# The first tokens' first four FFN tiles turned, rounded and subtracted between the last two output groups

## The chip, the cores and the metric

The kernel runs on one core of a Trainium2 chip. The metric is the time of one execution on the device, in microseconds (us). TensorE multiplies matrices into PSUM, whose eight banks are `bank[0]` to `bank[7]`; VectorE, ScalarE and GpSimd do the rest; SyncE (SP) issues the DMAs. Each engine works through its own queue in order, and the queues meet at semaphores alone. Called "granted clock" below is the share of TensorE's full clock that the chip let through.

## The reference

256 tokens of width 1024 in float32 go through two blocks. The first has three mixing branches and 32 experts; the second is attention and a gated feed-forward layer (FFN). The change lies between the last two steps of the second block:

```python
def second_block(x, g_pre_mix, g_post_mix, w_qkv, w_o, rel_bias, g_pre_ffn, g_post_ffn, w_gate, w_up, w_down):
    for i in range(DEPTH):
        h = rms_norm_2(x, g_pre_mix[i])
        ...
            m = chunk_relpos_attention(h, w_qkv[i], w_o[i], rel_bias[i // N_MIXERS])
        ...
        x = x + rms_norm_2(m, g_post_mix[i])
        h = rms_norm_2(x, g_pre_ffn[i])
        x = x + rms_norm_2(swiglu(h, w_gate[i], w_up[i], w_down[i]), g_post_ffn[i])
    return x

def rms_norm_2(x, g):
    xf = x.astype(jnp.float32)
    y = xf * lax.rsqrt(jnp.mean(xf * xf, axis=-1, keepdims=True) + RMS_EPS)
    return (y * g.astype(jnp.float32)).astype(x.dtype)

def swiglu(h, w_gate, w_up, w_down):
    return (jax.nn.silu(h @ w_gate) * (h @ w_up)) @ w_down
```

## The kernel before, in words

Tokens are split into two halves, i = 0 (first tokens) and i = 1 (second tokens), 128 each. Every float32 product is made of three faster ones: each operand is the sum of a rounded part ("hi", written by ScalarE) and a remainder ("lo", a subtraction by VectorE), and the product keeps hi x hi, lo x hi and hi x lo. Weights stream in pieces of 128 x 1024; `split_to(n)` splits the pieces up to number n, on ScalarE a cast (L1543, "wh"), on VectorE a subtraction (L1969, "wl"). Four pieces are held at a time, so a split also waits until TensorE is done with an older piece.

**The output product.** `o_tile(k, parts)` multiplies tile k of the attention's result with the rows k of `w_o`. A part (i, c) is the token half i and the column half c (512 columns); it sums into `bank[2 * c + i]` over the eight tiles, three matmuls of 512 columns for each (L782). The first tokens' parts are made first, tile by tile beside the attention. What is left at the end are tiles 5, 6 and 7 for the second tokens: nine matmuls for (1, 0), then nine for (1, 1) (L1412 to L1414).

**The norm and the sum.** For each part ScalarE squares the bank (L1552, with a read of the accumulator), VectorE multiplies the bank with the gain (`gained`, L2514). Once both column halves of a token half are squared, ScalarE adds their sums (`mean`, L1560), and GpSimd makes the factor (L2690, L2692). VectorE then adds the normed part to the residual X (`added`, L2521).

**The turn.** X is turned so that features lie on the partitions: `turn_ffn(i, tiles)` on TensorE turns 128 x 128 tiles (L1424) into the banks named by `FFN_BANK`, one tile each, and before tiles 0 and 4 it waits for `added` of the column half they lie in. ScalarE rounds each tile with the FFN's gain (L1914, "hi ffn"), VectorE subtracts (`low_ffn`, L2505, "lo ffn"). The norm of the FFN's input is applied later, to the products.

**The first gate product.** `first_gate` makes the first two of the FFN's gate groups: the first tokens' half tile by tile (`gate_half(0, ...)`, two matmuls of 256 columns, L1441), each behind "lo ffn" of its tile, then the second tokens' half (four matmuls, L1441 and L1445). The other turns stand between them as the table `later` says: the first tokens' tiles 5 to 7 behind gate tile 1, the second tokens' tiles 0 to 3 behind gate tile 5, and so on. Ahead of the gate half stand five turns and a filler, `warm(WARM[2], 4)`: six matmuls of a constant into bank 4, 12 records in the profile (L745). Then come the up product (`joint`, L848 and L851) and ten more chunks of the FFN.

The order on the other engines is written out by hand. ScalarE: the squares of (0,0) and (0,1), a mean, the square of (1,0), `split_to(q_o + 2)`, the square of (1,1), a mean, the roundings of the eight tiles of the first tokens, `split_to(q_o + 3)`, the roundings of the second tokens (q_o is the last piece of `w_o`; q_o + 1 and q_o + 2 hold the first gate group's weights). VectorE, in `add_normed`: gained (0,0), gained (0,1), added (0,0), gained (1,0), added (0,1), gained (1,1), four subtractions, added (1,0), four subtractions, added (1,1), then the second tokens' subtractions with the splits. Here the first index is the token half.

Of the kernel before, what the change touches and what calls it, by code (L numbers as in the profile page):

```python
# [13 lines left out]
ACT = mybir.ActivationFunctionType  # L14
AX = mybir.AxisListType.X

P = 128
# [13 lines left out]
WARM = (10, 1, 6, 10, 2, 6, 12)  # L31
FFN_BANK = ((0, 2, 6, 7, 1, 3, 0, 2), (6, 7, 1, 3, 0, 2, 3, 1))
# [13 lines left out]
G_MIX, G_MEM, G_Q, G_KV, G_POOL, G_MIX2, G_FFN2, G_ROUTE, G_FIN, G_EXP, G_END = np.cumsum([0, 8, 8, 3, 2, 4, 8, 8, 8, 8, 8]).tolist()  # L46
# [24 lines left out]
class Points:  # L71
# [10 lines left out]
    def up(self, name, *key):  # L82
        if name not in self.sems:
            self.sems[name] = self.semaphore("p_" + name.replace(" ", "_"))
        n = self.count[name] = self.count.get(name, 0) + 1
        assert self.real or (name, key) not in self.value, (name, key)
        self.value[name, key] = n
        self.latest = (self.sems[name], n)
        return self.sems[name], 1

    def at(self, name, *key):
        return (self.sems[name], self.value[name, key]) if self.real else (None, 1)
# [236 lines left out]
def program(nc, ctx, x, xT, mem, memT, positions, gate_b, grow, w_route, b_route, rel_ext, cst, out, wt, dense,  # L329
# [402 lines left out]
    def tensor(e, real):  # L732
# [8 lines left out]
        def warm(n, b, src=None):  # L741
            src = C if src is None else src
            enter(b)
            for _ in range(n):
                e.matmul(bank[b][:, 0:P], src[:, 0:P], src[:, 0:P], start=True, stop=True)  # L745
# [645 lines left out]
        def o_tile(k, *parts):  # L1391
            wide(wt.run["o", k // 2][k % 2], "gained o", (mT[0][:, k, :], mT[1][:, k, :]), k == 0, k == 7,
                 at("finished", "r", k), *parts)
# [15 lines left out]
            for k, i in HALVES_AT.get(step, ()):  # L1409
                o_tile(k, ((i, 0), (i, 1)))  # L1410
        o_tile(7, ((0, 0), (0, 1)))
        for c in range(2):  # L1412
            for k in (5, 6, 7):
                o_tile(k, ((1, c),))  # L1414


        def turn_ffn(i, *tiles):

            for k in tiles:
                b = FFN_BANK[i][k]  # L1420
                enter(b, "lo", "ffn", k, i)
                if k % 4 == 0:
                    e.wait_ge(*at("added", "o", i, k // 4))
                e.transpose(bank[b][:, P * i:P * i + P], X[:, i, P * k:P * k + P], ident).then_inc(*up("turn", "ffn", k, i))  # L1424

        def token_half(v, i):
            return v.rearrange("p (z n) -> p z n", z=2)[:, :, P * i:P * i + P]
# [22 lines left out]
        def first_gate():  # L1450

            later = {(0, 1): (0, 5, 6, 7), (0, 5): (1, 0, 1, 2, 3), (1, 0): (1, 4, 5, 6, 7)}
            turn_ffn(0, 0, 1, 2, 3, 4)
            warm(WARM[2], 4)
            for i in range(2):
                for q in wt.run["fg", 0]:
                    for kk in range(wt.pieces[q].rows):
                        gate_half(i, q, kk)
                        step = (i, wt.pieces[q].k0 + kk)
                        if step in later:  # L1460
                            turn_ffn(*later[step])
# [66 lines left out]
    def scalar(e, real):  # L1528
        split, limit_q = [0], [LATE]

        def split_to(n):

            while split[0] <= min(n, limit_q[0] - 1):
                q = split[0]
                p = wt.pieces[q]
                if p.first == 0:
                    e.wait_ge(*landed(p.unit))
                if q == LATE:
                    for u in under_split.values():
                        e.wait_ge(*released(u))  # L1540
                if q >= PIECES:
                    e.wait_ge(*at("piece", max(z for z in range(q) if wt.place(z) == wt.place(q))))
                e.copy(halves(q)[0], piece_view(q)).then_inc(*up("wh", q))  # L1543
                split[0] += 1
# [345 lines left out]
        for step, _ in enumerate(attention("r", 16, 384, causal_exps("r"), r_finish, 6, PT4)):  # L1890
# [6 lines left out]
            if step == 10:  # L1897
                whole(fill)
        q_o = wt.run["o", 3][1]
        for i in range(2):  # L1900
            for c in range(2):
                if (i, c) == (1, 1):
                    split_to(q_o + 2)
                e.wait_ge(*(at("piece", q_o) if (i, c) == (1, 1) else at("piece", q_o, i, c)))
                if (i, c) != (0, 0):
                    e.wait_ge(*own())
                square(rms("o")[0][:, 2 * c + i:2 * c + i + 1], bank[2 * c + i][:, :], junk, "o", c, i, scale=1 / 32)
            mean("o", i)


        for i in range(2):
            for k in range(8):
                e.wait_ge(*at("turn", "ffn", k, i))
                e.activation(hT[0][:, k, P * i:P * i + P], bank[FFN_BANK[i][k]][:, P * i:P * i + P], ACT.Copy,  # L1914
                             scale=G[:, G_FFN2 + k:G_FFN2 + k + 1]).then_inc(*up("hi", "ffn", k, i))
            if i == 0:
                split_to(q_o + 3)
        for i in range(2):
            e.wait_ge(*at("added", "o", i, 1))
            e.wait_ge(*(at("squared", "ffn", 0) if i else at("squared", "o", "mean", 1)))  # L1920
# [39 lines left out]
    def vector(e, real):  # L1960
        split, limit_q = [0], [LATE]

        def split_to(n):

            while split[0] <= min(n, limit_q[0] - 1):
                q = split[0]
                h, l = halves(q)
                e.wait_ge(*at("wh", q))
                e.tensor_tensor(l, piece_view(q), h.bitcast(F), ALU.subtract).then_inc(*up("wl", q))  # L1969
                split[0] += 1  # L1970
# [529 lines left out]
        def low_ffn(i, tiles):  # L2500

            sl = slice(P * i, P * i + P)
            for k in tiles:
                e.wait_ge(*at("hi", "ffn", k, i))
                e.scalar_tensor_tensor(hT[1][:, k, sl], bank[FFN_BANK[i][k]][:, sl], G[:, G_FFN2 + k:G_FFN2 + k + 1],  # L2505
                                       hT[0][:, k, sl].bitcast(F), ALU.mult, ALU.subtract).then_inc(*up("lo", "ffn", k, i))

        def add_normed(name, row, ready):

            e.wait_ge(*ready)  # L2510

            def gained(i, c):
                e.wait_ge(*at("squared", name, c, i))
                e.tensor_tensor(H[:, i, 512 * c:512 * c + 512], bank[2 * c + i][:, :],  # L2514
                                gb[:, row, 512 * c:512 * c + 512], ALU.mult).then_inc(*up("gained " + name, i, c))

            def added(i, c):
                xs = X[:, i, 512 * c:512 * c + 512]
                e.wait_ge(*at("gained " + name, i, c))
                e.wait_ge(*at("factor", name, i))  # L2520
                e.scalar_tensor_tensor(xs, H[:, i, 512 * c:512 * c + 512], rms(name)[1][:, i:i + 1], xs, ALU.mult,  # L2521
                                       ALU.add).then_inc(*up("added", name, i, c))

            gained(0, 0)
            gained(0, 1)
            added(0, 0)
            gained(1, 0)
            added(0, 1)
            gained(1, 1)
            if name == "o":  # L2530
                low_ffn(0, range(4))
            added(1, 0)
            if name == "o":
                low_ffn(0, range(4, 8))
            added(1, 1)
# [244 lines left out]
```

## Time and profile before

| | |
|---|---|
| median of 3 runs | 764.17 us (763.53 to 764.65) |
| profiled execution, its time | 765.39 us |
| its span, first to last instruction | 763.5 us |
| mean granted clock | 0.993 |
| TensorE busy | 728.5 us, 95% |
| VectorE busy | 417.9 us, 55% |
| ScalarE busy | 338.3 us, 44% |

The span is the time from the first to the last instruction; some 1.9 us of the profiled time lie outside. A row of the line of time gives start, duration, engine, line, operation, output and inputs by the program's names, the shape and how many instructions were merged; in brackets how long the engine stood before and what ended that. TensorE's matmuls overlap: the next one starts before the last one's recorded end, so distances between starts say more than recorded lengths.

### The profile page before, as it was taken

To read this page: it belongs to the slowest core of one execution; us is meant where nothing else is said; L and a number is where in the kernel's file an instruction comes from. 1 tells how busy PE (TensorE), PEld (TensorE's weight loads), DVE (VectorE), ACT (ScalarE), POOL (GpSimd) and SP (SyncE) were. 2 spreads that over 40 slices of the span, in tenths; PEclk is the share of its full clock that TensorE was granted. 3 is DMA by queue.
4 is the path that set the end of the run, shared out by engine and by line. 5 is a ranking of instruction groups with operands and counts; after the bars stand their busy time and mean duration, and the time that the engine had idled before them with its cause. 6 is when DMAs were issued, how large, how long until landed. Compare 5 with 4: busy or idle time off the path is not lost.

```text
span 763.5 us, 12333 instructions
## 1 busy us (share of the span) xinstructions
PE 728.5 (95%) x5082; PEld 596.0 (78%) x5082; DVE 417.9 (55%) x740; ACT 338.3 (44%) x605; POOL 32.8 (4%) x66
## 2 busy tenths in 40 slices
PE   9999999999999999999787789999999999999997
PEld 8998987888888866666455459998778888888885
DVE  5677656677666511111010118676568867676766
ACT  5966665554443521111010137555667453444343
POOL 1700000000000000000000001000001000000001
PEclk9999999999999999999999999999999999999999
DMA  8963667438989999999999997954234555545101
GB/s 333 418 232 120 227 212 283 174 128 319 364 320 346 377 412 420 422 426 424 427 424 424 419 415 313 419 176 161 111 111 166 192 194 178 209 170 209 62 1 55
DMA packets 30281, 206.05 MB, mean 270 GB/s; under 512 B 3600, under 2 KB 3984, under 8 KB 11408
## 3 DMA queue, kind: packets, MB, share of 16 engines
q1 hardware_dynamic: 30224, 205.25, 68.7%
q8 instruction: 41, 0.67, 0.4%
q14 instruction: 16, 0.13, 0.1%
HBM read 204.18 MB, written 1.05 MB: 269 GB/s over the span
## 4 chain that ended last, share of the span: by engine, by line
PE 87%; DMA 6%; ACT 2%; DVE 2%; issue 1%; POOL 0%; SPq 0%; DVEq 0%; POOLq 0%; ACTq 0%
PE ps L782 44%; PE ps L848 10%; DMA ext<-in_dense 6%; PE ps L1210 6%; PE ps L851 5%; PE ps L1231 3%; PE ps L1132 3%; PE ps L1241 2%; PE ps L888 1%; PE ps L1046 1%; PE ps L1356 1%; ACT big L1804 1%; PE ps L1370 1%; PE ps L1331 1%; PE ps L1261 1%
## 5 line engine op out<-in xcount | busy, mean ns | idle before, releaser
L1969 DVE TENSOR_TENSOR whl<-raw,whl 128x1024 fp32r<-128x1024 f32 (+4 forms) x182 | 213.0, 1189 | 127.6 <-ACT whl L1543 126.0
L1543 ACT CAST whl<-raw 128x1024 fp32r<-128x1024 f32 (+4 forms) x182 | 181.9, 1020 | 68.7 <-PE ps L782 46.7
L782 PE MATMUL ps<-whl,fra 128*128 128x512 f32 (+2 forms) x858 | 198.7, 387 | 0.0
L782 PEld LDWEIGHTS ps<-whl,fra 128*128 128x128 f32 x858 | 156.7, 188 | 30.4 <-issue 1.0
L848 PE MATMUL ps<-fra,whl 128*128 128x512 f32 x336 | 105.5, 395 | 0.0
L782 PE MATMUL ps<-whl,frb 128*128 128x512 f32 x360 | 84.9, 390 | 0.0
L782 PEld LDWEIGHTS ps<-whl,frb 128*128 128x128 f32 x360 | 66.6, 188 | 13.2
L851 PEld LDWEIGHTS ps<-fra,whl 128*128 128x128 f32 x336 | 63.1, 188 | 14.8
L782 PE MATMUL ps<-fra,whl 128*128 128x256 f32 x552 | 69.5, 285 | 0.0
L782 PEld LDWEIGHTS ps<-fra,whl 128*128 128x128 f32 x552 | 67.1, 191 | 0.8 <-issue 0.7
L851 PE MATMUL ps<-fra,whl 128*128 128x256 f32 x336 | 66.0, 278 | 0.0
L848 PEld LDWEIGHTS ps<-fra,whl 128*128 128x128 f32 x336 | 51.8, 189 | 0.7
L1210 PE MATMUL ps<-ext,big 128*32 128x256 f32 x320 | 46.6, 402 | 1.5 <-DMA big<-in_w_gate_e 1.4
L2398 DVE TENSOR_TENSOR S<-S,ps 128x256 f32<-128x256 f32 x6 | 2.5, 421 | 82.7 <-ACT S L1818 82.7
L1210 PE MATMUL ps<-raw,big 128*32 128x256 f32 x380 | 40.9, 389 | 7.0 <-DMA ext<-in_dense 3.8
L1210 PE MATMUL ps<-big 128*32 128x256 f32 x240 | 41.4, 396 | 4.1 <-DMA ext<-in_dense 4.1
L1818 ACT ACTIVATE S<-ps 128x256 f32<-128x256 f32 x6 | 2.3, 384 | 89.9 <-PE ps L1210 89.9
L1210 PEld LDWEIGHTS ps<-raw,big 128*32 128x32 f32 x380 | 21.4, 112 | 16.6 <-issue 9.9
L2547 DVE TENSOR_REDUCE S<-ps 128x256 f32<-128x512 f32 x44 | 28.2, 683 | 4.2 <-PE ps L851 4.2
L1617 ACT ACTIVATE S<-S,st 128x128 f32<-128x128 f32 (+1 forms) x48 | 21.5, 450 | 16.1 <-DVE st L2052 16.1
L1210 PEld LDWEIGHTS ps<-ext,big 128*32 128x32 f32 x320 | 22.6, 116 | 7.2 <-issue 2.8
L1210 PEld LDWEIGHTS ps<-big 128*32 128x32 f32 x240 | 19.9, 114 | 10.4 <-issue 5.8
(300 smaller groups left out, 856.9 us busy)
## 6 DMA issues: line engine op xcount, KB each, us to landing
raw<-in_dense SPq DMA_DIRECT2D x79, 1024.0 KB, 5.2
ext<-in_dense SPq DMA_DIRECT2D x11, 2048.0 KB, 24.2
raw<-in_dense SPq DMA_DIRECT2D x5, 2048.0 KB, 31.1
ext<-in_w_down_e SPq DMA_DIRECT2D x8, 1024.0 KB, 9.5
big<-in_w_gate_e SPq DMA_DIRECT2D x7, 1024.0 KB, 27.3
big<-in_dense SPq DMA_DIRECT2D x3, 2048.0 KB, 29.1
raw<-in_dense SPq DMA_DIRECT2D x2, 3072.0 KB, 33.2
raw<-in_w_gate_e SPq DMA_DIRECT2D x5, 1024.0 KB, 7.6
```

The source lines that it names most:

```text
L782: t = e.matmul(o, a, w, start=first and n == 0, stop=final and n == 2, skip_group_check=not check)
L848: e.matmul(bank[b][:, :], h[:, kk, cols[j]], hT_both[:, k], start=(k == 0), stop=(k == 7), skip_group_check=True)
L851: t = e.matmul(bank[b][:, 0:256], l[:, kk, cols[j]], hT[0][:, k], start=False, stop=(k == 7), skip_group_check=True)
L888: t = e.matmul(bank[j // 2][:, 256 * (j % 2):256 * (j % 2) + 256], w[:, kk, P * j:P * j + P], y[:, k], start=(n == k == j % 2 == 0), stop= ...
L1132: t = e.matmul(bank[2 + a][:, P * (kk % 4):P * (kk % 4) + P], H[:, i, P * kk:P * kk + P], hot[:, P * i:P * i + P], start=(i == 0), stop=(i ...
L1210: t = e.matmul(bank[0][32 * j:32 * j + 32, 256 * half_:256 * half_ + 256], XE[:, kk, 32 * j:32 * j + 32], expert_rows(key, 4 * g + j, kk), ...
L1231: t = e.matmul(bank[2 + c][32 * j:32 * j + 32, :], hidden(g)[1][:, P * k + 32 * j:P * k + 32 * j + 32], slot_view(wt.raws["ed", 4 * g + j] ...
L1241: t = e.matmul(turned(k), rows_out(g, k // 4)[:, P * (k % 4):P * (k % 4) + P], CM, start=False, stop=False, skip_group_check=True)
L1543: e.copy(halves(q)[0], piece_view(q)).then_inc(*up("wh", q))
L1617: t = e.activation(s, s, ACT.Exp, bias=mx(h)[:, i:i + 1], scale=-1.0, accum_out=sums(h)[0][:, i:i + 1])
L1969: e.tensor_tensor(l, piece_view(q), h.bitcast(F), ALU.subtract).then_inc(*up("wl", q))
L2547: e.tensor_reduce(dst[:, j, :], bank[b][:, :].rearrange("p (z n) -> p n z", z=2), AX, ALU.add).then_inc(*up("summed " + name, c, j))
```

## The change

Four of the five turns of the first tokens move from behind the output parts to between (1,0) and (1,1), the fifth stays behind (1,1), and the filler is gone. On ScalarE the four roundings move ahead of the square of (1,1), and the split of piece q_o + 2 moves from ahead of that square to behind the rounding of the fifth tile. On VectorE the four subtractions move ahead of the gained product of (1,1). Nothing that is computed changes, except that the six filler matmuls, whose result nobody reads, are left out.

```diff
@@ TensorE
         o_tile(7, ((0, 0), (0, 1)))
-        for c in range(2):
-            for k in (5, 6, 7):
-                o_tile(k, ((1, c),))
...
+        for c in range(2):
+            if c:
+                turn_ffn(0, 0, 1, 2, 3)
+            for k in (5, 6, 7):
+                o_tile(k, ((1, c),))
...
             later = {(0, 1): (0, 5, 6, 7), (0, 5): (1, 0, 1, 2, 3), (1, 0): (1, 4, 5, 6, 7)}
-            turn_ffn(0, 0, 1, 2, 3, 4)
-            warm(WARM[2], 4)
+            turn_ffn(0, 4)
@@ ScalarE
+        def high_ffn(k, i):
+            e.wait_ge(*at("turn", "ffn", k, i))
+            e.activation(hT[0][:, k, P * i:P * i + P], bank[FFN_BANK[i][k]][:, P * i:P * i + P], ACT.Copy,
+                         scale=G[:, G_FFN2 + k:G_FFN2 + k + 1]).then_inc(*up("hi", "ffn", k, i))
+
         for i in range(2):
             for c in range(2):
                 if (i, c) == (1, 1):
-                    split_to(q_o + 2)
+                    for k in range(4):
+                        high_ffn(k, 0)
...
-        for i in range(2):
-            for k in range(8):
...
-            if i == 0:
-                split_to(q_o + 3)
+        high_ffn(4, 0)
+        split_to(q_o + 2)
+        for k in range(5, 8):
+            high_ffn(k, 0)
+        split_to(q_o + 3)
+        for k in range(8):
+            high_ffn(k, 1)
@@ VectorE
             added(0, 1)
-            gained(1, 1)
             if name == "o":
                 low_ffn(0, range(4))
+            gained(1, 1)
             added(1, 0)
```

## Rows read from the trace of the kernel before

**Rows 1.** The page, part 1: busy time, share of the span and instructions of each engine

```profile
PE 728.5 (95%) x5082; PEld 596.0 (78%) x5082; DVE 417.9 (55%) x740; ACT 338.3 (44%) x605; POOL 32.8 (4%) x66
```

**Rows 2.** TensorE's waits, whole run: us in total, times, longest

```profile
PE ps L1210 <- DMA ext<-in_dense: 7.8, 2, 4.1
...
PE ps L1441 <- DVE fra L2505: 0.3, 2, 0.2
```

**Rows 3.** The waits of all engines from 580 us to the end

```profile
POOL st L2690 <- ACT junk L1552: 172.6, 2, 172.1
```

**Rows 4.** The chain that ended last: start, us, what

```profile
571.39 0.69 DVE H L2514
```

**Rows 5.** TensorE's line of time, 560 to 584 us: start, us, what

```profile
563.52 7.12 PE L782 MATMUL ps<-whl,fra 128*128 128x512 f32 x30
570.48 0.71 PE L1424 MATMUL ps<-C,X 128*128 128x128 f32 x5
571.02 1.50 PE L745 MATMUL ps<-C 128*128 128x128 f32 x12
572.49 0.71 PE L1441 MATMUL ps<-fra,whl 128*128 128x256 f32 x4
...
574.18 0.71 PE L1441 MATMUL ps<-fra,whl 128*128 128x256 f32 x4 [0.18 <-DVE fra L2505]
...
575.97 0.47 PE L1441 MATMUL ps<-fra,whl 128*128 128x256 f32 x2 [0.17 <-DVE fra L2505]
```

**Rows 6.** VectorE's line of time, the same stretch

```profile
568.45 0.75 DVE L2521 SCALAR_TENSOR_TENSOR X<-H,st,X 128x512 f32<-128x512 f32 x1 [0.36 <-POOL st L2692]
...
569.96 0.74 DVE L2521 SCALAR_TENSOR_TENSOR X<-H,st,X 128x512 f32<-128x512 f32 x1
571.39 0.69 DVE L2514 TENSOR_TENSOR H<-ps,gb 128x512 f32<-128x512 f32 x1 [0.69 <-ACT junk L1552]
...
573.03 0.74 DVE L2521 SCALAR_TENSOR_TENSOR X<-H,st,X 128x512 f32<-128x512 f32 x1
573.69 1.12 DVE L2505 SCALAR_TENSOR_TENSOR fra<-ps,C,fra 128x128 fp32r<-128x128 f32 x4
574.73 0.74 DVE L2521 SCALAR_TENSOR_TENSOR X<-H,st,X 128x512 f32<-128x512 f32 x1
575.47 1.13 DVE L2505 SCALAR_TENSOR_TENSOR fra<-ps,C,fra 128x128 fp32r<-128x128 f32 x4
```

**Rows 7.** ScalarE's line of time, the same stretch

```profile
567.40 0.29 ACT L1560 ACTIVATE st<-st 128x1 f32<-128x1 f32 x1
...
571.39 0.29 ACT L1560 ACTIVATE st<-st 128x1 f32<-128x1 f32 x1
571.59 1.38 ACT L1914 ACTIVATE fra<-ps,C 128x128 fp32r<-128x128 f32 x5
...
574.12 1.06 ACT L1543 CAST whl<-raw 128x1024 fp32r<-128x1024 f32 x1
575.05 1.16 ACT L1914 ACTIVATE fra<-ps,C 128x128 fp32r<-128x128 f32 x4
```

**Rows 8.** TensorE's line of time in the expert stage, two places

```profile
400.49 0.42 PE L1210 MATMUL ps<-raw,big 128*32 128x256 f32 x3 [1.68 <-DMA big<-in_w_gate_e]
...
443.81 0.47 PE L1219 MATMUL ps<-C,S 128*128 128x128 f32 x2 [1.05 <-DVE S L2398]
445.73 0.66 PE L1261 MATMUL ps<-ext,S 128*32 128x256 f32 x4 [1.45 <-issue]
```

**Rows 9.** Stretches: us, busy by engine, PEclk (granted clock), DMA share, GB/s

```profile
397.00:401.00 4.00, 2.33 (x21) 1.68 (x23) 0.00 (x0) 0.00 (x0) 0.00 (x0) 1.00 1.01 428
410.00:416.00 6.00, 4.90 (x64) 2.79 (x64) 0.00 (x0) 0.00 (x0) 0.00 (x0) 0.72 0.99 418
442.50:449.50 7.00, 4.50 (x51) 2.44 (x47) 0.42 (x1) 1.50 (x4) 0.00 (x0) 0.76 1.00 415
570.00:577.00 7.00, 6.65 (x52) 6.03 (x51) 6.31 (x18) 5.67 (x18) 0.56 (x1) 1.00 0.01 2
```

More of the change, by code:

```diff
@@ L1908, in scalar @@
             mean("o", i)
-        for i in range(2):
-            for k in range(8):
-                e.wait_ge(*at("turn", "ffn", k, i))
-                e.activation(hT[0][:, k, P * i:P * i + P], bank[FFN_BANK[i][k]][:, P * i:P * i + P], ACT.Copy,
-                             scale=G[:, G_FFN2 + k:G_FFN2 + k + 1]).then_inc(*up("hi", "ffn", k, i))
-            if i == 0:
-                split_to(q_o + 3)
+        high_ffn(4, 0)
[5 more added lines that the diff above has]
+            high_ffn(k, 1)
         for i in range(2):
```

## The prediction, made before the changed kernel was built or run

> **What bounds the kernel now.** I read the page first. TensorE is busy 728.5 us of 763.5 [rows 1], so whatever moves its work at this place moves the end, unless a wait further on takes it back. The list of TensorE's waits over the whole run has the two waits of this stage at 0.3 us together, on the subtraction at L2505 [rows 2]. The same list for 580 us to the end has no row of TensorE at all; its rows are other engines that wait, the first ones shown [rows 3]. So from 580 us on TensorE runs without waiting for anybody, and a shift that exists at 580 arrives at the end unchanged. The chain that ended last shows who sets the time in the stage itself: behind the 30 output matmuls of TensorE, which end at 563.52 + 7.12 = 570.64 [rows 5], and a square on ScalarE it goes on VectorE from 571.39 [rows 4] until the second tokens' gate matmuls start.
>
> TensorE's line of time gives the shapes [rows 5]. Its matmuls are recorded with 0.27 to 0.39 us each but overlap, so I count from start to start. 30 output matmuls take 570.48 - 563.52 = 6.96 us, 0.232 each; 9 of them are one column half of the last three tiles, 2.09 us. So the half for the second tokens and the first 512 columns, called (1,0), hands over at 570.48 - 2.09 = 568.39, and (1,1) at 570.48. Five turns take 571.02 - 570.48 = 0.54, 0.108 each. The second tokens' gate matmuls, which need everything, start at 575.97: that is the point I measure the change at.
>
> VectorE sets that point [rows 6]: from the gained product of (1,1) at 571.39, four subtractions, the addition at 573.03, four subtractions from 573.69, the addition at 574.73, the first subtraction of the second tokens at 575.47, and 0.50 later TensorE. Four subtractions with the next start cost 574.73 - 573.69 = 1.04; an addition before a subtraction costs 573.69 - 573.03 = 0.66 or 575.47 - 574.73 = 0.74.
>
> **The change, part by part.**
>
> The wait in front of the first turn. The four turns for the first tokens now stand between (1,0) and (1,1), and the first waits for the addition (0,0) on VectorE. That addition starts at 568.45 and takes 0.75 [rows 6]: it ends at 569.20. Nothing ahead of it changes: it follows ScalarE's mean at 567.40 [rows 7] by 1.05 us over GpSimd's root. TensorE answers to a VectorE result about 0.15 after its end (the subtraction that starts at 573.69 ends some 0.35 later and lets the gate matmul start at 574.18; 0.49 in all, once more 0.50 at 575.47 [rows 5, 6]). So the turns start at 569.35, and not at 568.39: 0.96 us of new standing time, with nine output matmuls, (1,1), queued behind the waiting turn. The banks that the turns write are free by then.
>
> The turns. Four times 0.108 = 0.43. (1,1) therefore starts at 569.78 and hands over at 571.87 instead of 570.48: 1.39 later. On the path it costs all of that, because ScalarE's square of (1,1), the mean, GpSimd's root and the gained product hang on its last matmul.
>
> The filler and the turns that went. The 12 matmul records from 571.02 to 572.49 are gone [rows 5]. I cost this at nothing either way: they lie beside the first four subtractions, the first gate matmul started at 572.49 when the first of these had just ended, and TensorE stands anyway ahead of 574.18 and of 575.97.
>
> The moved subtractions. The first four now run ahead of the gained product of (1,1). They follow the addition (0,1) at 569.96 [rows 6], from about 570.6 to 571.7, time in which VectorE would now be standing; their roundings on ScalarE (0.25 each, from about 569.7) are ahead of them. This takes 1.03 us (four of about 0.26) out of the chain behind (1,1). That is the gain of the change, and its cover is complete.
>
> A wait that comes up. With the four subtractions gone from behind the gained product, the addition (1,0) comes to its factor too early. For the first tokens the addition followed the mean by 568.45 - 567.40 = 1.05 [rows 6, 7]. The mean of the second tokens moves from 571.39 to 572.78 [rows 7]; so the addition starts at 573.83, not at 573.4 when VectorE is free: 0.4 us of the 1.03 are lost again.
>
> The sum. Mean 572.78, addition (1,0) 573.83, fifth subtraction 574.49, addition (1,1) 575.53, first subtraction of the second tokens 576.27, gate matmul of the second tokens 576.77. Before it was 575.97: **+0.80 us**. By terms: +0.96 wait, +0.43 turns, -1.03 subtractions, +0.44 for the factor. TensorE itself doesn't set it: after (1,1) come one turn and the gate matmuls of four tiles with three turns until about 573.3, it then stands until 574.98 (fifth subtraction at 574.49 and 0.49), works 1.4 us, and stands again from 576.4.
>
> ScalarE's moved cast. The cast of 1024 columns for the second piece after the last output tile (L1911) stood ahead of the square of (1,1), and now stands behind it. From the mean at 572.78: 0.20 to the fifth rounding (571.59 - 571.39), 0.25, cast 0.93 (575.05 - 574.12), three roundings 0.75, second cast 0.93 [rows 7]: the first rounding of the second tokens starts at 575.84 and ends 0.37 later, at 576.21. The subtraction that needs it would start at 576.27. The cover is 0.06 us; without it, if both casts held ScalarE for their full 1.06, the path would be 0.2 longer. I take nothing, and keep the 0.2 for the range. The subtraction of the same piece on VectorE stays behind the second tokens' four subtractions, so it moves with the rest, and so does the release of its buffer: TensorE meets the piece with the same slack. SP's queue issues nothing in this stretch that TensorE waits for [rows 3].
>
> What a turn costs in a stream: the row gives 0.108 each for five in a row [rows 5]. The Trainium skill, "TensorE: Matmul & The Clock Gate", Part 4: PE-mode transpose, has about 275 ns for one in the context of a kernel; the recorded length here, 0.27, agrees with it, and the distance between two does not. With 0.275 for each of the four, my estimate would be 0.67 longer, +1.5 us.
>
> **The rivals.**
>
> A, the wait in front of the turns isn't there, or the change doesn't hold what it says: if the turns found their addition done, the shift of (1,1) would be 0.43 alone, and the sum 0.43 - 1.03 + 0.44 = -0.16: 764.0 us. If the factor weren't late either, -0.6: 763.6. Against it: the addition's start at 568.45 has its cause in work that isn't touched. Even this case stays within 0.2%; to be faster by more than that, 1.5 us would have to go from a chain of which at most 1.03 is moved.
>
> B, the clock falls (the side of slower). The granted clock was 1.00 in this stage [rows 9], which is the level of 2.4 GHz, and the filler is gone, with two new standing times of 1.0 and 1.7 us. Elsewhere it fell to 1.2 GHz: around 411, behind the longest wait of TensorE, 4.1 us for a transfer [rows 2, 9], and around 445, where it had only two identity matmuls at 443.81 between waits of 1.05 and 1.45 us [rows 8, 9]. Against it: ahead of 400.49 it stood 1.68 us between column-tiled matmuls and kept 1.00 [rows 8, 9]. In the new stretch from 573.3 to 576.8 it would have eight gate matmuls and four turns, which is more than at 443.81 and not far from the other. A fall costs this: 6 us at a mean of 0.72 is 6 x 0.28 = 1.7 us of full-clock work [rows 9]. It decides if the stretch with the 1.7 us wait counts as rest: then 0.80 + 1.7 = +2.5 us, 766.7 us, and less if the fall meets time in which TensorE stands.
>
> The Trainium skill speaks against this change here, in the same section: in transpose mode the array isn't counted as busy the way it is in a matmul. By that, the eleven turns between the output and the second gate half keep nothing up, and B is likelier. The trace's fall at 445, around two such short matmuls, doesn't contradict it.
>
> C, ScalarE becomes the bound: the two casts at 1.06 and roundings that wait for the turns put 0.2 to 0.5 on the sum: 765.2 to 765.5 us.
>
> D, the shift is absorbed later: 764.2 us. Against it: no wait of TensorE after 580 [rows 3].
>
> **How the numbers follow.** The sum is made in the profiled execution: 765.39 us, of which the span is 763.5; +0.80 makes 766.2 there. The median of the runs is 764.17, 1.2 below the profiled one, and +0.80 gives 764.97. Chances: the forecast 0.58, C 0.14, A with D 0.14, B 0.14. A difference of 0.2%, 1.5 us, is about what a measurement of this kernel can tell from no change. The forecast, A, C and D lie inside it; the three runs before spread over 1.1 us, so some of the forecast's chance goes to each side. Faster 0.05, same 0.77, slower 0.18. The range takes A's 763.9 or so, C and half of B: 763.8 to 766.5.
>
> **What would show it.** In the changed kernel: TensorE's first turn at about 569.35 behind a wait on the addition at L2521; (1,1)'s square on ScalarE at about 572.05; the addition (1,0) behind GpSimd at 573.8; the first gate matmul with the fifth tile at about 575.0; the second tokens' gate half at 576.8; the same clock as before. A gate half before 576 would make the forecast wrong; so would a stretch of half clock after 573, or a wait of TensorE after 580 that was not there.

## The result

The changed kernel takes 765.65 us in the median of 11 runs (764.47 to 768.85) against 764.09 of 11 runs before; the ratio is 1.0021, with a 95% interval of 1.0011 to 1.0031. Measured again beside other kernels it was 1.0009 (0.9998 to 1.0021) and 1.0016 (1.0006 to 1.0025). So it is slower, by 0.1 to 0.2%. The profiled execution took 765.13 us with a span of 763.2.

All distances below are from one mark, the start of VectorE's first addition, (0,0), to the second tokens' first gate matmul. Everything ahead of the mark is the same in both programs. TensorE's line of time after the change answers to [rows 5]; the turns stand at L1419 now and the gate matmuls at L1443. The first row ends with the half (1,0):

```profile
562.38 5.07 PE L782 MATMUL ps<-whl,fra 128*128 128x512 f32 x21
568.21 0.63 PE L1419 MATMUL ps<-C,X 128*128 128x128 f32 x4 [0.76 <-DVE X L2528]
568.60 2.31 PE L782 MATMUL ps<-whl,fra 128*128 128x512 f32 x9
570.75 0.27 PE L1419 MATMUL ps<-C,X 128*128 128x128 f32 x1
570.78 0.71 PE L1443 MATMUL ps<-fra,whl 128*128 128x256 f32 x4
572.41 0.55 PE L1419 MATMUL ps<-C,X 128*128 128x128 f32 x3 [0.92 <-DVE H L2521]
...
573.87 0.71 PE L1443 MATMUL ps<-fra,whl 128*128 128x256 f32 x4 [0.44 <-DVE fra L2512]
...
575.67 0.47 PE L1443 MATMUL ps<-fra,whl 128*128 128x256 f32 x2 [0.17 <-DVE fra L2512]
```

VectorE, which answers to [rows 6] (addition L2528, gained product L2521, subtraction L2512):

```profile
567.32 0.75 DVE L2528 SCALAR_TENSOR_TENSOR X<-H,st,X 128x512 f32<-128x512 f32 x1 [0.36 <-POOL st L2699]
...
568.82 0.74 DVE L2528 SCALAR_TENSOR_TENSOR X<-H,st,X 128x512 f32<-128x512 f32 x1
569.48 1.12 DVE L2512 SCALAR_TENSOR_TENSOR fra<-ps,C,fra 128x128 fp32r<-128x128 f32 x4
571.67 0.69 DVE L2521 TENSOR_TENSOR H<-ps,gb 128x512 f32<-128x512 f32 x1 [1.07 <-ACT junk L1553]
572.71 0.75 DVE L2528 SCALAR_TENSOR_TENSOR X<-H,st,X 128x512 f32<-128x512 f32 x1 [0.35 <-POOL st L2699]
573.38 1.12 DVE L2512 SCALAR_TENSOR_TENSOR fra<-ps,C,fra 128x128 fp32r<-128x128 f32 x4
574.41 0.74 DVE L2528 SCALAR_TENSOR_TENSOR X<-H,st,X 128x512 f32<-128x512 f32 x1
575.18 1.12 DVE L2512 SCALAR_TENSOR_TENSOR fra<-ps,C,fra 128x128 fp32r<-128x128 f32 x4
```

ScalarE, which answers to [rows 7] (mean L1561, roundings L1903, square L1553, casts L1544):

```profile
566.27 0.29 ACT L1561 ACTIVATE st<-st 128x1 f32<-128x1 f32 x1
...
568.55 1.14 ACT L1903 ACTIVATE fra<-ps,C 128x128 fp32r<-128x128 f32 x4 [0.37 <-PE ps L1419]
570.95 0.60 ACT L1553 ACTIVATE junk<-ps 128x512 f32<-128x512 f32 x1 [1.25 <-PE ps L782]
...
571.67 0.29 ACT L1561 ACTIVATE st<-st 128x1 f32<-128x1 f32 x1
...
572.12 1.04 ACT L1544 CAST whl<-raw 128x1024 fp32r<-128x1024 f32 x1
...
573.82 1.06 ACT L1544 CAST whl<-raw 128x1024 fp32r<-128x1024 f32 x1
574.75 1.16 ACT L1903 ACTIVATE fra<-ps,C 128x128 fp32r<-128x128 f32 x4
```

GpSimd, the factor of the second tokens:

```profile
572.04 0.56 POOL L2699 TENSOR_TENSOR st<-st 128x1 f32<-128x1 f32 x1 [3.56 <-ACT st L1561]
```

Two cuts of the span say where the time is. First the kernel before, then the changed one, each from the mark to the second gate half and from there to the end (us; busy time of TensorE, its weight loads, VectorE, ScalarE, GpSimd; granted clock, DMA share, GB/s):

```profile
568.45:575.97 7.52, 7.17 (x50) 6.29 (x49) 6.68 (x16) 6.63 (x19) 0.78 (x2) 1.00 0.01 2
575.97:763.50 187.53, 181.84 (x976) 156.29 (x976) 135.03 (x160) 83.58 (x105) 5.06 (x9) 1.00 0.40 146
```

```profile
567.32:575.67 8.35, 6.06 (x38) 4.97 (x38) 6.77 (x16) 6.52 (x19) 0.78 (x2) 1.00 0.01 2
575.67:763.20 187.53, 181.83 (x976) 156.27 (x976) 135.08 (x160) 83.55 (x105) 5.05 (x9) 1.00 0.40 146
```

The stretch grew from 7.52 to 8.35 us (8.36 before its two ends are rounded, as in the table below), and the rest is 187.53 us in both. Nothing of the shift is taken back in the 187 us that follow, and nothing is added. The span as a whole is 0.3 us shorter in this execution, because the mark came at 567.32 instead of 568.45. That difference lies ahead of the first changed instruction; in the later profiles, of whatever kernel, the mark stood anywhere from 566.60 to 569.68. A reader who compares two spans here compares the expert stage of two executions. A reader who measures from the mark gets the distance of the changed kernel again to 0.01 us, in every repeat below.

### The profile page after: what moved, and what is told of

It is laid out like the page before. It is cut to its first block, busy times and chain, and to the rows that moved or that the text cites. A ratio compares the mean times of both kernels' runs of the same rounds, so it can differ in the third digit from the quotient of the medians.

```text
span 763.2 us, 12309 instructions
## 1 busy us (share of the span) xinstructions
PE 727.2 (95%) x5070; PEld 594.9 (78%) x5070; DVE 417.9 (55%) x740; ACT 338.1 (44%) x605; POOL 32.2 (4%) x66
## 4 chain that ended last, share of the span: by engine, by line
PE 85%; DMA 8%; SPq 3%; ACT 1%; issue 1%; DVE 1%; POOL 0%; DVEq 0%; POOLq 0%; ACTq 0%
PE ps L782 45%; PE ps L848 10%; DMA ext<-in_dense 5%; PE ps L851 5%; PE ps L1210 5%; DMA raw<-in_w_up_e 2%; SPq L609 2%; PE ps L1241 2%; PE ps L1231 2%; PE ps L1132 2%; PE ps L888 2%; PE ps L1046 1%; PE ps L1356 1%; PE ps L1331 1%; PE ps L1370 1%
## 5 line engine op out<-in xcount | busy, mean ns | idle before, releaser
L1544 ACT CAST whl<-raw 128x1024 fp32r<-128x1024 f32 (+4 forms) x182 | 181.8, 1019 | 68.4 <-PE ps L782 46.6
L1210 PE MATMUL ps<-ext,big 128*32 128x256 f32 x320 | 48.2, 414 | 1.6 <-DMA big<-in_w_gate_e 1.5
L1210 PE MATMUL ps<-raw,big 128*32 128x256 f32 x380 | 42.5, 398 | 6.4 <-DMA ext<-in_dense 3.9
```

The lines of the kernel that those rows point to most:

```text
L1210: t = e.matmul(bank[0][32 * j:32 * j + 32, 256 * half_:256 * half_ + 256], XE[:, kk, 32 * j:32 * j + 32], expert_rows(key, 4 * g + j, kk), ...
```

## The experiments

Two theories are set against each other in what was expected of each run. Theory W: the waits and turns alone make the loss. Theory C: the granted clock falls in this stage because the filler is gone. Every run was read in the same way; the distance from the mark, in us, with the start of the square of (1,1) and of the addition (1,0) after the mark. Each distance is that of the one profiled execution:

| run | what | distance | square (1,1) | addition (1,0) | ratio to before (95%) |
|---|---|---|---|---|---|
| before | | 7.52 | 2.22 | 4.58 | |
| after | the change | 8.36 | 3.63 | 5.40 | 1.0021 (1.0011 to 1.0031) |
| a4_after | the same again | 8.36 | 3.63 | 5.40 | 1.0009 (0.9998 to 1.0021) |
| c2_after | the same again | 8.37 | 3.64 | 5.40 | 1.0016 (1.0006 to 1.0025) |
| b5_tensor | TensorE's part alone | 8.91 | 3.63 | 5.99 | 1.0019 (1.0009 to 1.0029) |
| a2_late | turns two tiles later | 7.61 | 2.88 | 4.64 | 1.0012 (0.9999 to 1.0024) |
| a3_bare | before, no filler | 7.49 | 2.22 | 4.58 | 0.9997 (0.9987 to 1.0006) |
| a1_fill | filler, too much of it | 8.99 | 3.64 | 5.40 | 1.0017 (1.0006 to 1.0027) |
| c1_fill | filler that fits | 8.37 | 3.64 | 5.40 | 1.0019 (1.0010 to 1.0028) |
| b3_cast | cast at its old place | 9.13 | 4.44 | 6.20 | one run |
| b4_back | two subtractions back | 8.39 | 3.64 | 5.49 | one run |
| b1_two | two tiles early | 7.27 | 2.52 | 4.36 | 1.0001 (0.9990 to 1.0011) |
| c3_three | three tiles early | 7.46 | 2.78 | 4.54 | one run |
| d1_length | the change, filler elsewhere | 8.36 | 3.63 | 5.40 | 1.0016 (1.0006 to 1.0026) |

The time from the second gate half to the end was 187.51 to 187.54 us in every one of them.

**The change again.**

> The changed kernel once more, as the mark for the other runs of this batch. The distance from the start of the addition (0,0) on VectorE to the second tokens' first gate matmul was 7.52 us before and 8.35 us in the changed kernel. Theory W (waits alone): 8.35 again and +0.8 us in time. Theory C (the clock falls here in some executions, because the filler is gone): the distance is 8.35 in most executions and the time is +1.5 us, with single executions 2 us or more above the rest.

> The changed kernel a third time, as the mark for the next one. Theory W: distance 8.36 us, time 0.84 us (0.11%) over before; the three measurements together should lie around 1.001. Theory C: nearer to 1.002.

The distance is 8.36 and 8.37. The times don't choose between the two theories by themselves: 1.0009 and 1.0016.

**TensorE's part alone.** Before, with this alone:

```diff
+        for c in range(2):
+            if c:
+                turn_ffn(0, 0, 1, 2, 3)
+            for k in (5, 6, 7):
+                o_tile(k, ((1, c),))
...
-            turn_ffn(0, 0, 1, 2, 3, 4)
-            warm(WARM[2], 4)
+            turn_ffn(0, 4)
```

> The change on TensorE alone: four turns between the last two output groups, no filler, but ScalarE and VectorE in their order of before (roundings behind the square of (1,1), subtractions behind its gained product). Theory W (the sum of the prediction): the wait and the turns stay on the path, 0.96 + 0.43, and nothing comes back, so the distance from the addition (0,0) to the second tokens' gate half is 7.52 + 1.39 = 8.91 us, 0.55 more than in the changed kernel, and the time is 1.4 us (0.18%) over before. A rival that has the loss come from the new order on ScalarE and VectorE expects it at or under 8.36.

8.91 us, as expected to the hundredth. VectorE has its four subtractions between the gained product and the addition again (b5_tensor, L2514, L2505, L2521), and the addition doesn't wait for the factor:

```profile
570.95 0.69 DVE L2514 TENSOR_TENSOR H<-ps,gb 128x512 f32<-128x512 f32 x1 [2.10 <-ACT junk L1552]
571.55 1.12 DVE L2505 SCALAR_TENSOR_TENSOR fra<-ps,C,fra 128x128 fp32r<-128x128 f32 x4
572.59 0.74 DVE L2521 SCALAR_TENSOR_TENSOR X<-H,st,X 128x512 f32<-128x512 f32 x1
```

So TensorE's part costs 1.39 and the new order on VectorE and ScalarE gives 0.55 back: the addition (1,0) comes 0.59 earlier, which is the four subtractions (1.03) less what is lost to the factor (0.44), and 0.04 of that goes again at ScalarE's cast, which the section on the prediction works out.

**The turns two tiles later.** The changed kernel with

```diff
-            if c:
-                turn_ffn(0, 0, 1, 2, 3)
             for k in (5, 6, 7):
+                if (c, k) == (1, 7):
+                    turn_ffn(0, 0, 1, 2, 3)
                 o_tile(k, ((1, c),))
```

> The changed kernel with the four turns two tiles later: behind tiles 5 and 6 of the last column half instead of ahead of tile 5. The addition they wait for is then done 0.4 us before TensorE comes to them. Theory W: the standing time of 0.96 us goes, the last output matmul ends 0.43 later than before the change instead of 1.39, and the distance is 7.52 + 0.43 - 1.03 + 0.44 = 7.36 us, 0.99 less than in the changed kernel and 0.16 less than before it; time 1.0 us under the changed kernel. Theory C: the same distance, and a time that still lies 0.5 us or more above before, since the long wait ahead of the fifth gate tile and the missing filler stay.

The wait is gone: TensorE's row has no standing time in front of the turns, and the distance falls by 0.75. But 0.25 of the expected 0.99 didn't come. TensorE, then ScalarE (a2_late):

```profile
568.93 0.60 PE L1419 MATMUL ps<-C,X 128*128 128x128 f32 x4
```

```profile
569.24 1.14 ACT L1903 ACTIVATE fra<-ps,C 128x128 fp32r<-128x128 f32 x4 [0.79 <-PE ps L1419]
570.47 0.60 ACT L1553 ACTIVATE junk<-ps 128x512 f32<-128x512 f32 x1
```

The instruction behind the last output matmul starts at 570.07, 2.48 us after the mark at 567.59, and the square could start 0.2 later, at 2.67. It starts at 2.88: ScalarE is still in the four roundings that stand ahead of it in its queue (569.24 + 1.14 = 570.38). Work put ahead of a wait is free only where it ends before the wait does; in the changed kernel it did, because TensorE's own wait had held the square back anyway.

**The filler.** Two ways to look at the clock. Before without its filler:

```diff
             turn_ffn(0, 0, 1, 2, 3, 4)
-            warm(WARM[2], 4)
```

> The kernel before without its filler ahead of the gate product, nothing else changed. Theory W: the filler lay under the wait for the first subtraction, so the distance stays 7.5 us and the time is that of before within 0.1 us. Theory C: the distance stays, and the time rises by 0.5 us or more in the median, with slow single executions.

Distance 7.49, ratio 0.9997, granted clock 1.00 in the stage. The filler of the kernel before bought nothing here; its own price was 0.03 us. And the changed kernel with filler ahead of the turns and of the first tokens' fifth gate tile:

```diff
             if c:
+                warm(3, 4)
                 turn_ffn(0, 0, 1, 2, 3)
...
                     for kk in range(wt.pieces[q].rows):
+                        if (i, wt.pieces[q].k0 + kk) == (0, 4):
+                            warm(6, 6)
                         gate_half(i, q, kk)
```

> The changed kernel with filler under its two new waits: 3 filler matmuls (0.7 us) ahead of the four turns and 6 (1.5 us) ahead of the first tokens' fifth gate tile, both shorter than the waits they lie under (0.94 and 1.7 us). Theory W: nothing changes, distance 8.3 to 8.4, time as the changed kernel within 0.1 us. Theory C: the distance is the same, but the time comes down by 0.7 us to +0.8 us over before, and the slow single executions go.

This one missed: the distance grew to 8.99. The wait of 1.7 us under which the six matmuls were to lie doesn't exist at that place (a1_fill, TensorE and ScalarE):

```profile
573.17 1.50 PE L745 MATMUL ps<-C 128*128 128x128 f32 x12
574.43 0.72 PE L1444 MATMUL ps<-fra,whl 128*128 128x256 f32 x4
574.99 0.60 PE L1419 MATMUL ps<-C,X 128*128 128x128 f32 x4
```

```profile
575.30 1.14 ACT L1906 ACTIVATE fra<-ps,C 128x128 fp32r<-128x128 f32 x4 [0.53 <-PE ps L1419]
```

The filler keeps TensorE until 574.43, the gate matmuls follow at once with no wait, and the second tokens' turns come so late that ScalarE waits 0.53 us for them. In the changed kernel's rows the reason can be read: TensorE stands at 572.41, for 0.92 us, and what ends it is the gained product of (1,1), not the subtraction. The turn of tile 5 writes bank 3, and bank 3 holds the output half (1,1) until VectorE has read it. Only 0.44 us of standing are left at the fifth gate tile. With filler sized by these rows, against the run above:

```diff
-                            warm(6, 6)
+                            warm(2, 6)
                         gate_half(i, q, kk)
                         step = (i, wt.pieces[q].k0 + kk)
+                        if step == (0, 1):
+                            warm(4, 6)
                         if step in later:
                             turn_ffn(*later[step])
```

> The changed kernel with filler that fits under each of its new waits as the trace has them: 3 matmuls ahead of the four turns (0.7 us under 0.94), 4 ahead of the turn of the sixth tile (1.0 under 1.1), 2 ahead of the fifth gate tile (0.5 under 0.7). Theory W: distance 8.4 us, time within 0.1% of the changed kernel in this batch. Theory C: distance the same, time 0.5 us or more under the changed kernel.

```profile
572.87 1.05 PE L745 MATMUL ps<-C 128*128 128x128 f32 x8
...
574.81 0.61 PE L745 MATMUL ps<-C 128*128 128x128 f32 x4
575.40 0.71 PE L1444 MATMUL ps<-fra,whl 128*128 128x256 f32 x4
```

The distance is 8.37 again, and the time isn't lower than that of the changed kernel in its batch (1.0019 against 1.0016). The clock theory falls: neither does filler bring anything back, nor does a profile of any of these kernels show less than 1.00 in this stage. A profile is one execution, but each execution also lists its mean granted clock. The 35 executions of the changed kernel have 0.9930 on average, those of before in two of the same batches 0.9930 and 0.9929. A fall like the one around 411 us (6 us at 0.72) takes 0.0022 off that mean, and an average of 35 is uncertain by 0.0003, so the clock didn't fall in the stage in all or most of them. In the changed kernel's profile the second row is the stage; the first is the fall in the expert stage that both kernels have, which answers to [rows 9]:

```profile
410.00:416.00 6.00, 5.66 (x67) 3.64 (x68) 0.00 (x0) 0.26 (x1) 0.00 (x0) 0.72 0.98 414
...
566.00:577.00 11.00, 8.70 (x55) 7.18 (x54) 9.05 (x21) 7.76 (x24) 1.34 (x3) 1.00 0.01 1
```

**ScalarE's cast at its old place.** The changed kernel with

```diff
                 if (i, c) == (1, 1):
+                    split_to(q_o + 2)
                     for k in range(4):
                         high_ffn(k, 0)
...
         high_ffn(4, 0)
-        split_to(q_o + 2)
```

> The changed kernel with ScalarE's cast of the piece q_o + 2 back ahead of the first rounding, its old place. Theory W: the cast fits under TensorE's second half of output matmuls, ScalarE isn't the bound in the changed kernel, and the distance stays at 8.36 us. The rival (ScalarE with its cast moved behind the square sets the time): the distance falls by 0.2 us or more.

Both expectations missed: 9.13, 0.77 worse. The cast didn't start at 569.5 (b3_cast, ScalarE: cast, roundings, square):

```profile
570.87 1.05 ACT L1544 CAST whl<-raw 128x1024 fp32r<-128x1024 f32 x1 [1.39 <-PE ps L782]
571.83 1.14 ACT L1903 ACTIVATE fra<-ps,C 128x128 fp32r<-128x128 f32 x4
573.05 0.60 ACT L1553 ACTIVATE junk<-ps 128x512 f32<-128x512 f32 x1
```

The buffer it writes is held by an older piece, that of output tile 5, until the last half has used it. Before the change that was the case three matmuls after (1,0); now the turns and their wait stand in between, so the cast starts 2.25 us after the mark, the roundings behind it, and the square of (1,1) at 4.44 instead of 3.63. Moving the cast behind the square is no choice of taste in this change. Where it stands now it costs 0.02 to 0.04 us, which the section on the prediction works out.

**Two of the four subtractions back.** The changed kernel with

```diff
             if name == "o":
-                low_ffn(0, range(4))
+                low_ffn(0, range(2))
             gained(1, 1)
+            if name == "o":
+                low_ffn(0, range(2, 4))
             added(1, 0)
```

> The changed kernel with two of the four moved subtractions put back behind the gained product of (1,1). Theory W: in the changed kernel VectorE stands 0.35 us for GpSimd's factor ahead of the addition (1,0), so two subtractions of 0.26 there cost next to nothing: the gained product at 4.35 after the mark, 0.61 and 0.52 later the addition at 5.48 instead of 5.40, and a distance of 8.44 us. If the factor isn't what the addition waits for, two subtractions cost their 0.52: 8.88 us.

8.39 (8.44 expected): two subtractions put back on the path cost 0.03 us, not 0.52. The addition follows them at once, without the 0.35 us of waiting that it has in the changed kernel:

```profile
573.33 0.60 DVE L2512 SCALAR_TENSOR_TENSOR fra<-ps,C,fra 128x128 fp32r<-128x128 f32 x2
573.85 0.74 DVE L2528 SCALAR_TENSOR_TENSOR X<-H,st,X 128x512 f32<-128x512 f32 x1
```

It starts 0.09 later than in the changed kernel, and only 0.03 of that arrives, because the second tokens' first subtraction, which sets the end, waits for ScalarE's rounding in both. So of the four moved subtractions two were worth next to nothing: without them VectorE reaches the addition earlier and stands there for the factor.

**Two tiles early.** Built from before: turns 0 and 1 between tiles 6 and 7 of the last half, two roundings ahead of the square, two subtractions ahead of the gained product, the cast where it was before, no filler:

```diff
         for c in range(2):
             for k in (5, 6, 7):
+                if (c, k) == (1, 7):
+                    turn_ffn(0, 0, 1)
                 o_tile(k, ((1, c),))
...
-            turn_ffn(0, 0, 1, 2, 3, 4)
-            warm(WARM[2], 4)
+            turn_ffn(0, 2, 3, 4)
```

> A version built from the sum: only two tiles are turned early, between tiles 6 and 7 of the last output half, where the addition is done; their roundings (0.5 us) then end about when the square of (1,1) can start, and two subtractions ahead of the gained product leave as many behind it as the factor takes. No filler. Theory W: square of (1,1) at 2.44 to 2.5 after the mark, turns 0.22, subtractions -0.52, no wait for the factor: distance 7.22 us, 0.30 less than before and 1.14 less than in the changed kernel; time 0.3 us (0.04%) under before, which a timing can't tell from none. The rival, by which any turn between the output groups costs more than it brings: 7.5 us or more.

7.27 us, 0.25 less than before and 1.09 less than the change; in time 1.0001 (0.9990 to 1.0011), which can't be told from before. ScalarE gets the cast, two roundings and the square in without a gap, and VectorE reaches the addition when the factor is there:

```profile
567.90 1.05 ACT L1543 CAST whl<-raw 128x1024 fp32r<-128x1024 f32 x1
568.85 0.62 ACT L1902 ACTIVATE fra<-ps,C 128x128 fp32r<-128x128 f32 x2
569.56 0.60 ACT L1552 ACTIVATE junk<-ps 128x512 f32<-128x512 f32 x1
```

```profile
570.28 0.69 DVE L2519 TENSOR_TENSOR H<-ps,gb 128x512 f32<-128x512 f32 x1 [0.43 <-ACT junk L1552]
570.89 0.60 DVE L2510 SCALAR_TENSOR_TENSOR fra<-ps,C,fra 128x128 fp32r<-128x128 f32 x2
571.41 0.74 DVE L2526 SCALAR_TENSOR_TENSOR X<-H,st,X 128x512 f32<-128x512 f32 x1
```

**Three tiles early.** The version with two, and one more of each:

```diff
                 if (c, k) == (1, 7):
-                    turn_ffn(0, 0, 1)
+                    turn_ffn(0, 0, 1, 2)
...
-                    for k in range(2):
+                    for k in range(3):
                         high_ffn(k, 0)
...
-                low_ffn(0, range(2))
+                low_ffn(0, range(3))
             gained(1, 1)
```

> As the version with two early tiles, but with three. By the chains as now read: the three roundings on ScalarE end 0.25 later and hold the square of (1,1) back to 2.72 after the mark (2.52 with two), the mean comes at 3.44, and with one subtraction left behind the gained product the addition (1,0) waits for its factor until 4.49 (4.36 with two). Theory W: distance 7.40 us, 0.13 more than with two. The rival, by which every subtraction moved ahead saves its 0.26: 7.0 us.

7.46, 0.19 more than with two. The third rounding ends at 571.61 and the square starts at 571.69, 2.78 after the mark:

```profile
570.73 0.88 ACT L1902 ACTIVATE fra<-ps,C 128x128 fp32r<-128x128 f32 x3
571.69 0.60 ACT L1552 ACTIVATE junk<-ps 128x512 f32<-128x512 f32 x1
```

## Why the prediction was right, and what it missed

The range held the time, and the sum was right where it can be read: +0.80 predicted from the mark on, +0.84 found. That 765.65 lies inside the range, 0.7 above the forecast, is luck in part: that much room upward had been left for a fall of the clock, which didn't come. Step by step, from the mark at 568.45 in [rows 6] and 567.32 after:

- *The wait in front of the turns*: predicted 0.96, from a start at 569.35, 0.90 after the mark. Found: 568.21, 0.89 after the mark. From start to start, one matmul at a time, TensorE loses 0.92 there; the 0.76 in brackets counts from a recorded end. Right.
- *The turns*: 0.43 and a square of (1,1) 1.39 later. Found 2.22 to 3.63, 1.41 later. The four turns take less, 568.60 - 568.21 = 0.39, and the nine output matmuls behind them more, 570.75 - 568.60 = 2.15 against 2.05 before; why these are slower is not shown. Right in the sum.
- *The subtractions*: 1.03 off the chain. b5_tensor has the chain with them in: its gained product starts at 570.95 and its addition at 572.59, 1.64 later. In the changed kernel this is 572.71 - 571.67 = 1.04. The 0.60 between is the 1.03 less the wait for the factor.
- *The factor*: predicted 0.44 lost, addition at 5.38 after the mark. Found 5.40; GpSimd's row and 0.35 of standing ahead of the addition show it, and b4_back prices it.
- *VectorE as the engine that sets the end, with ScalarE 0.06 under it* (rival C): wrong, and small; see below.
- *The filler at nothing*: right within 0.03; a3_bare has 7.49.
- *The clock* (rival B, 0.14) didn't occur: 1.00 in the stage in every profile, with or without filler. The prediction counted eleven turns between the output and the second gate half; there are eight behind the output and twelve from the mark on. The Trainium skill's sentence in "TensorE: Matmul & The Clock Gate", Part 4: PE-mode transpose, that a transpose doesn't count as busy in the same way, had no effect that could be seen here: with twelve turns, 25 other matmuls and no filler, 6.06 us busy of 8.35, the clock stayed at 1.00.
- *The price of a turn*: the start distance, predicted 0.108 and found 0.10, was the right one. With the 0.275 us that the Trainium skill gives there for one in context, the prediction's estimate for the whole sum was +1.5; found was +0.84.

**The last step.** The prediction had VectorE set the second gate half and gave ScalarE a cover of 0.06. The second tokens' first subtraction starts 0.03 after the end of ScalarE's rounding in all fourteen profiles, before the change too. The rounding by itself, in a narrow window so that the row isn't merged with the next three (before, the changed kernel, b4_back):

```profile
575.05 0.39 ACT L1914 ACTIVATE fra<-ps,C 128x128 fp32r<-128x128 f32 x1
574.75 0.39 ACT L1903 ACTIVATE fra<-ps,C 128x128 fp32r<-128x128 f32 x1
575.85 0.37 ACT L1903 ACTIVATE fra<-ps,C 128x128 fp32r<-128x128 f32 x1
```

The subtractions start at 575.47, 575.18 and 576.25. Where no rounding holds VectorE back, a subtraction follows an addition's start by 0.66 or 0.67 (573.03 to 573.69 before, 572.71 to 573.38 after); at this last step it is 0.74 before, 0.77 after and 0.71 in b4_back. The prediction took the 0.74 for VectorE's own pace. The chain that ends last here runs from the addition (1,0) over the fifth subtraction, two gate tiles and the turn on TensorE (574.42) to the rounding on ScalarE. In the changed kernel the cast that stands ahead of the rounding ends last: the rounding starts 0.93 after the cast's start at 573.82, the same distance as from the other cast to the next rounding, and 0.06 after the turn's end. In b5_tensor, b3_cast, b4_back, b1_two and c3_three the rounding starts 0.04 after the turn's end. Because both chains start at the same addition, the sum came out nearly right. ScalarE's share in the 0.84 is about 0.02, and 0.04 against a version in which the cast isn't in the way. a1_fill shows how little TensorE had to spare: its turn starts 0.67 later than in the changed kernel, and the distance grows by 0.63.

Two more things were off without harm to the sum. The prediction called the turns' banks free, which holds for the four early ones, and saw one wait of 1.7 us ahead of the fifth gate tile. The trace has two, 0.92 in front of the sixth tile's turn for bank 3 and 0.44 at the gate tile. The first of them was beside the path, because the fifth gate tile waits for its subtraction in either case, but the reading misled a1_fill. And the forecast's place within 0.2% was near its edge: the first measurement, 1.0021, is just outside.

The size is where the sum was short. The time rose by more than the stage: in the means of the executions by 1.9 (first measurement), 1.1 (a4_after) and 1.2 us (c2_after), each with an uncertainty of 0.3 to 0.5, against 0.84. Each run also lists its span, so its time can be split. The 98 executions of before in four batches have a mean span of 762.81 and lie 1.86 us outside it on average, 95 of them between 1.7 and 2.0, the other three up to 2.17. The changed kernel lies 2.48, 2.28 and 2.18 us outside in its three measurements, single executions up to 3.1. Its spans are 0.6 (a4_after) and 0.9 us (c2_after) longer than those of before in their batch, each with an uncertainty of 0.3, which agrees with the 0.84 of the stage. The other 0.3 to 0.4 us lie before the first or after the last instruction, which no profile covers. a2_late has it too: 0.09 more in distance, 0.8 more in time, 2.33 outside. a1_fill and c1_fill, with filler, lie 1.79 outside, but c1_fill's time isn't lower for it: its span is 1.45 over before, with an uncertainty of 0.33, where its distance explains 0.85. That led to the last run, the changed kernel with six more filler matmuls behind the expert part (L1303):

```diff
-WARM = (10, 1, 6, 10, 2, 6, 12)
+WARM = (10, 7, 6, 10, 2, 6, 12)
```

> The changed kernel with the six filler matmuls put back far ahead of the stage, at the end of the expert part (one filler matmul there becomes seven), so that TensorE's program has its old length. What is open: the executions of the changed kernel had a mean of 2.2 to 2.5 us outside the span from first to last instruction, those of the kernel before 1.85, and the two kernels with filler in the stage 1.79. If this follows from how many instructions TensorE's program has, the time outside falls back to 1.8 to 1.9; if it follows from the order in the stage, it stays at 2.2 or more. In both cases the distance in the stage is 8.36 us, and the filler costs up to 0.7 us of span where it stands now.

With six filler matmuls far from the stage the time outside is 1.82 us, and 1.83 for before in that batch; the distance is 8.36. So the extra doesn't come from the order in the stage alone. (The changed kernel without this filler wasn't run on the chip that d1_length ran on, so a difference between chips isn't excluded; before lay 1.83 to 1.89 outside on all four chips.) That it comes from the length of TensorE's program is not shown: b5_tensor (2.21), a2_late (2.33) and b1_two (2.07) are as short and have it, but a3_bare, just as short, has only 1.93. What in the layout of a program decides it stays open. d1_length gained nothing in time from it: its mean is 1.12 above before, its span 1.13 longer with an uncertainty of 0.3. How much of that is the filler's own time can't be told.

## What to carry to other kernels

Measure an edit from the last unchanged event ahead of it to the first event behind which both programs are alike: here that repeated to 0.01 us, while the times of one kernel scatter by 1 us, most of it from more than 100 us earlier. Work that is pulled ahead of a wait pays only up to the next wait behind it, so the size to move is the one that just fills the standing time (two tiles here, not four), at a point where its own input is already there. Before work is put in front of a wait on any engine, look at each buffer it writes and at who still reads it. And a step between two instructions of one engine may hide a wait that is too short for the view to name: compare it with the same step elsewhere (0.66 and 0.74 here).

## What the runs showed that was not expected

The time outside the span isn't a constant of the machine: 1.79 to 1.93 us in some programs with hardly any spread, 2.1 to 2.5 with single values of 3.1 in others that differ by 12 records of filler or by order alone. And the expert stage moves the whole program by up to 3.1 us between executions (mark at 566.60 in b5_tensor, at 569.68 in a3_bare), with one to three falls of the clock in it. The distance repeats to 0.01 and the rest of the span to 0.03, so the scatter of one kernel's span is that of the mark. Whether the falls make it is not shown.
